# A two-layer decoder trunk: the RMSNorm channel sum split over four column groups of the array, with a second product that adds the groups

## What is computed

```python
def _rmsnorm(x, g):
    xf = x.astype(jnp.float32)
    y = xf * lax.rsqrt(jnp.mean(xf * xf, axis=-1, keepdims=True) + EPS)
    return (y * g.astype(jnp.float32)).astype(x.dtype)

def _modulate(x, g, shift, scale):
    return _rmsnorm(x, g) * (1 + scale[:, None, :]) + shift[:, None, :]

for layer in range(DEPTH):
    h = _modulate(x, norm_g[layer, 0], shift, scale)    # norm 0, norm 2
    x = x + gate[:, None, :] * mixer(h)
    h = _modulate(x, norm_g[layer, 1], shift, scale)    # norm 1, norm 3
    x = x + gate[:, None, :] * _hier_moe(h, ...)
return _rmsnorm(x, final_g)                             # norm 4
```

## Time and profile before

| | us |
|---|---|
| median of 3 runs | 1664.53 (1662.39 to 1671.16) |
| the profiled execution | 1674.01 |
| its span, first to last instruction | 1672.5 |
| TensorE matmuls busy | 1472.2 (88%) |
| weight loads busy | 1028.0 (61%) |
| VectorE busy | 620.4 (37%) |
| ScalarE busy | 413.5 (25%) |
| POOL busy | 225.0 (13%) |
| mean granted TensorE clock | 0.906 |

### The profile page before, as it was taken

One profiled execution on the slowest core, in us unless ns is written; L12 is line 12 of the kernel. 1 busy time (PEld: TensorE's weight loads), 2 busy tenths in 40 slices (PEclk: granted clock), 3 DMA queues, 4 the chain that ended last, 5 costly groups with the idle time before them and its releaser, 6 DMA issues.

```text
span 1672.5 us, 19460 instructions
## 1 busy us (share of the span) xinstructions
PE 1472.2 (88%) x7272; PEld 1028.0 (61%) x7272; DVE 620.4 (37%) x1426; ACT 413.5 (25%) x843; POOL 225.0 (13%) x206
## 2 busy tenths in 40 slices
PE   5698998969799999998369999999996899999945
PEld 3345586654388777775235677666544777777733
DVE  2795736541232421111252003888512324211113
ACT  4214112130312122221110113667404121222202
POOL 5001200000002010000534590000000110000010
PEclk8689998989868999999679999999997699999976
DMA  9543323341765789887683663000005176998941
GB/s 239 160 151 51 71 76 101 124 129 51 236 241 176 301 321 329 325 326 254 154 101 104 199 200 126 1 2 2 1 0 226 42 284 241 334 345 316 327 161 51
DMA packets 131928, 287.61 MB, mean 172 GB/s; under 512 B 11959, under 2 KB 94251, under 8 KB 120044
## 3 DMA queue, kind: packets, MB, share of 16 engines
q1 hardware_dynamic: 110112, 232.80, 40.8%
q0 software_dynamic: 13456, 25.12, 7.4%
q10 hardware_dynamic: 8268, 28.46, 4.2%
HBM read 269.94 MB, written 30.93 MB: 180 GB/s over the span
## 4 chain that ended last, share of the span: by engine, by line
PE 78%; DVE 10%; issue 4%; DMA 3%; ACT 3%; POOL 1%; ACTq 0%; DVEq 0%; POOLq 0%
PE bank L772 18%; PE bank L518 12%; PE bank L784 9%; PE bank L697 7%; PE bank L506 3%; PE bank L766 2%; PE bank L709 2%; PE bank L882 2%; PE bank L474 2%; PE bank L910 2%; PE bank L894 2%; PE bank L641 2%; PE bank L820 2%; PE bank L452 1%; PE bank L724 1%
## 5 line engine op out<-in xcount | busy, mean ns | idle before, releaser
L518 PE MATMUL bank<-hT,ring 128*128 128x512 f32 x448 | 201.8, 613 | 23.6 <-ACT hT L1014 13.4
L772 PE MATMUL bank<-ring,arena 128*128 128x256 f32 x800 | 177.9, 379 | 0.0
L518 PEld LDWEIGHTS bank<-hT,ring 128*128 128x128 f32 x448 | 87.7, 197 | 134.1 <-issue 109.5
L772 PEld LDWEIGHTS bank<-ring,arena 128*128 128x128 f32 x800 | 150.1, 190 | 19.4
L772 PE MATMUL bank<-arena 128*128 128x256 f32 x672 | 152.1, 383 | 0.0
L1818 DVE SCALAR_TENSOR_TENSOR arena<-bank,arena 128x256 f32<-128x256 f32 x46 | 22.3, 484 | 325.4 <-ACT arena L1180 325.1
L772 PEld LDWEIGHTS bank<-arena 128*128 128x128 f32 x672 | 128.1, 193 | 16.9
L2051 POOL DMA_INDIRECT arena<-h_tokens,arena x46 | 50.1, 1090 | 568.9 <-PE bank L766 359.0
L697 PE MATMUL bank<-mixT,ring 128*128 128x512 f32 x256 | 110.4, 593 | 1.6 <-ACT mixT L1137 0.9
L784 PE MATMUL bank<-ring,arena 128*128 128x512 f32 x224 | 100.8, 593 | 3.2 <-issue 3.2
L1172 ACT ACTIVATE arena<-bank 128x512 f32<-128x512 f32 x92 | 55.0, 597 | 178.8 <-PE bank L766 102.2
(11 more groups left out here) (427 smaller groups left out, 2186.7 us busy)
## 6 DMA issues: line engine op xcount, KB each, us to landing
ring<-in_ada_w SPq DMA_DIRECT2D x48, 1024.0 KB
ring<-in_e_w_down SPq DMA_DIRECT2D x28, 1024.0 KB
ring<-in_e_w_up SPq DMA_DIRECT2D x26, 1024.0 KB
ring<-in_e_w_gate SPq DMA_DIRECT2D x24, 1024.0 KB
expert_rows<-arena ACTq DMA_DIRECT2D x46, 512.0 KB, 8.3
arena<-in_e_w_gate SPq DMA_DIRECT2D x22, 1024.0 KB
arena<-in_e_w_up SPq DMA_DIRECT2D x20, 1024.0 KB
arena<-in_e_w_down SPq DMA_DIRECT2D x18, 1024.0 KB
```

Of the source, the lines that this page charges most:

```text
L518: last = mm(bank(stage, i)[:, :], chunk(kind, m, c)[:, k, j * P:(j + 1) * P], hT[:, k, :], start=(k == 0), stop=(k == KD - 1))
L772: last = mm(b[:, CC * n:CC * n + CC], xgT[:, e % 2, k, :], chunk(w, l, e)[:, k, :], start=(k == 0), stop=(k == KD - 1))
```

## The change

Each norm takes two banks instead of one. The first product keeps its 8 products of one square each, but with a stationary operand of 32 columns, `first`, whose first column is ones and whose other columns are zero. Product `k` goes to column group `k % 4`, that is to PSUM partitions `32*(k%4)` to `32*(k%4)+31`, so that four partial sums come to lie in rows 0, 32, 64 and 96 and zeros in all other rows. ScalarE copies the bank into `rstd` (`sums`). A second product of `ones` with `rstd`, 128x512, adds the four rows and spreads the sum over all partitions; VectorE's `variance` reads it from the second bank.

```diff
-STAGES = [("x", KD), ("param", 1), ("adap", 1), ("norm0", 1), ("adap", 1), ...
+STAGES = [("x", KD), ("param", 1), ("adap", 1), ("norm0", 2), ("adap", 1), ...
...   the same for norm1 to norm4
+        first = sb("first", [P, 32])
...
             def norm(m):
                 wait_bank(pe, f"norm{m}")
-                b = bank(f"norm{m}")
                 for k in range(KD):
                     pe.wait_ge(S["sq_ready"], KD * m + k + 1)
-                    last = mm(b[:, :], ones[:, :], hT[:, k, :], start=(k == 0), stop=(k == KD - 1))
+                    g = k % 4
+                    last = mm(bank(f"norm{m}")[32 * g:32 * g + 32, :], first[:, :], hT[:, k, :], start=(k < 4), stop=(k >= 4),
+                              skip_group_check=True)
                 last.then_inc(fsem(f"norm{m}"), 1)
+
+            def norm_sum(m):
+                wait_bank(pe, f"norm{m}", 1)
+                pe.wait_ge(S["sum_ready"], m + 1)
+                mm(bank(f"norm{m}", 1)[:, :], ones[:, :], rstd[:, :], start=True, stop=True).then_inc(fsem(f"norm{m}", 1), 1)
 
             ada_rows(0)
             norm(0)
             ada_rows(1)
+            norm_sum(0)
...
             norm(1)
+            norm_sum(1)
             ada_rows(14)
...   norm_sum(m) right behind norm(m) for 2, 3 and 4 too
+            def sums(m):
+                wait_full(act, f"norm{m}")
+                AC(rstd[:, :], bank(f"norm{m}")[:, :], ACT.Copy).then_inc(S["sum_ready"], 1)
+                act.wait_ge(S["sum_ready"], m + 1)
+                nc.scalar.nop().then_inc(rsem(f"norm{m}"), 1)
...
             ada_row(0)
+            sums(0)
             act.wait_ge(S["dve_s5"], 2)
...
                     AC(hT[:, k, :], xT[:, k, :], ACT.Square).then_inc(S["sq_ready"], 1)
+                sums(m)
                 act.wait_ge(S["var_ready"], m + 1)
...
-                wait_full(dve, st)
-                link(V.tensor_scalar(rstd[:, :], bank(st)[:, :], 1.0 / D, EPS, ALU.mult, ALU.add))
-                signal(rsem(st))
+                wait_full(dve, st, 1)
+                link(V.tensor_scalar(rstd[:, :], bank(st, 1)[:, :], 1.0 / D, EPS, ALU.mult, ALU.add))
+                signal(rsem(st, 1))
                 signal(S["var_ready"])
...
             link(G.memset(ones[:, :], 1.0))
+            link(G.memset(first[:, :], 0.0))
+            link(G.memset(first[:, 0:1], 1.0))
```

More of the change, by code:

```diff
@@ L44 @@
 MAGIC = 12582912.0
-STAGES = [("x", KD), ("param", 1), ("adap", 1), ("norm0", 1), ("adap", 1), ("ct", 2), ("fvec", 2), ("adap", 2), ("ada0", 1),
+STAGES = [("x", KD), ("param", 1), ("adap", 1), ("norm0", 2), ("adap", 1), ("ct", 2), ("fvec", 2), ("adap", 2), ("ada0", 1),
           ("u", 4), ("adap", 2), ("ada0g", 1), ("gates", 1), ("s5_e", 8), ("u2", 8), ("ut", 4), ("s5_g", 8), ("qk", 4),
@@ L54 @@
           ("mls", 1 + NT), ("adap", 1), ("o", 4), ("ada1_4", 1), ("mlh", 2), ("adap", 1), ("mly", 4), ("ada1_5", 1),
-          ("mlt", MH), ("aout", 8), ("adap", 2), ("norm1", 1), ("adap", 2)]
+          ("mlt", MH), ("aout", 8), ("adap", 2), ("norm1", 2), ("adap", 2)]
 NPRE = 8
@@ L88 @@
 WIDE = [sum(1 for x in STEPS[:n + 1] if x[1] > 1) for n in range(NI)]
-STAGES += [("norm2", 1), ("nkc", 4), ("ngate", 1), ("nq", 8), ("chid", 4), ("nks", 2), ("kcmp", 1), ("vcmp", 1), ("nvs", 4),
+STAGES += [("norm2", 2), ("nkc", 4), ("ngate", 1), ("nq", 8), ("chid", 4), ("nks", 2), ("kcmp", 1), ("vcmp", 1), ("nvs", 4),
            ("cscore", NT), ("nkw", 2), ("ctr", 2), ("nvw", 4), ("ctr", 2), ("ada3", 1)]
-STAGES += [("as", 2 * NI, (0, 1, 2, 3)), ("at", len(PTILE), (4, 5)), ("ao", NH // 2, (6, 7)), ("nout", KD), ("norm3", 1)]
+STAGES += [("as", 2 * NI, (0, 1, 2, 3)), ("at", len(PTILE), (4, 5)), ("ao", NH // 2, (6, 7)), ("nout", KD), ("norm3", 2)]
 STAGES += moe_stages(1) + moe_stages2(1)
-STAGES += [("norm4", 1), ("xo", 8)]
+STAGES += [("norm4", 2), ("xo", 8)]
 TILE, USES, _next = {}, [0] * 8, 0
@@ L304, in build @@
         free = [sem(f"bank_free{i}") for i in range(8)]
-        names = ["x_in", "raw_in", "dt_in", "c_in", "small_in", "twiddle", "rows_ready", "rows_used", "const_ready", "x_ready", "par_ready", "sil_ready", "mod_ready",
+        names = ["x_in", "raw_in", "dt_in", "c_in", "small_in", "twiddle", "rows_ready", "sum_ready", "rows_used", "const_ready", "x_ready", "par_ready", "sil_ready", "mod_ready",
                  "pow_ready", "e_ready", "et_ready", "g_ready", "m_in", "sq_ready", "h_part", "h_ready",
@@ L800, in _ @@
             norm(2)
+            norm_sum(2)
             pe.wait_ge(S["h_ready"], KD * 3)
@@ L916, in _ @@
             norm(3)
+            norm_sum(3)
             route(1)
@@ L919, in _ @@
             norm(4)
+            norm_sum(4)
             for i in range(8):
```

## The result

| | before | changed |
|---|---|---|
| median of 17 runs each | 1666.74 (1662.39 to 1679.96) | 1678.11 (1671.45 to 1680.74) |
| ratio, 95% interval | | 1.0047 [1.0027, 1.0067] |
| profiled execution / span | 1674.01 / 1672.5 | 1679.77 / 1677.9 |

A forecast was written before the change was run, and what follows sets the result against it. The chain of waits bounds the kernel, TensorE holding 78%. Gains of 3.2 + 1.9 + 0.3 + 0.3 in norms 1, 4, 3, 2, less 0.3 for memsets, give 5.4 us: 1664.53 to 1659.1, range 1653 to 1667.

The forecast's parts named there:

- The first product: Norm's 16 passes in column groups: 3.6 us at the low clock with squares ready; otherwise 4.7 (high) or 5.6 (low).
- the question of the waits: First product: assumed a product may start beside another group's although a wait on its square stands between; no row showed it.
- in order: Rival, chance 0.13: everything behind a waiting pass of the first product waits too, 9 slots instead of 4; gain 0.1, 1664.4.
- alone: Rival, chance 0.07: each wait lets a product start only when the array is empty; 10.2 us slower, 1674.7.
- Copy and second product: In each norm ScalarE's copy costs 0.8 us with handovers, the second product 1.03 (high clock) or 2.07 (low).
- Norm 0: 12 us of slack hide the sum; `sums(0)`, now ahead of the two Sin, stays just hidden, cost 0.
- Norms 3 and 4: Sum ends earlier: norm 3 by 0.3 us (0.6 gain to 0.5 loss), norm 4 by 1.9 (1.4 to 2.4).
- Norm 2: Sum ends 1.4 to 2.4 us earlier, but VectorE's operations meet POOL's; gain 0.3 us (-0.5 to +2.4).
- POOL gives way: Rival, chance 0.12: in norm 2 VectorE's eight operations keep their pace against POOL; norm 2 gains 4.6 us, 1654.8 in all.
- They still end about when the reciprocal does: Norm 1: TensorE's `ada_rows(14)` and `(15)`, 3.66 us behind the new wait, end with the reciprocal; norm 1 gain 3.2 us.
- Can the lower column work cost clock?: Asked of the norms' products; answer: work in four column groups raises the clock, second product taken as high half the time.
- 2 us either way: Expert stage: its 32 transposes and 64 gate products may meet either clock by luck, moving single norms by 2 us.

The follow-up runs named there:

- kept busy: Changed kernel plus 16 unread products of 128 columns between ada_rows(15) and the transposes after norm 1: 1664.94, ratio 0.9957 to the kernel before.
- paced: Changed kernel plus two unread products of 128 columns for each tile VectorE normalises in norms 1 and 3: 1660.6, ratio 0.9896 to the kernel before.
- the moved copies: Changed kernel with only ScalarE's ada_row(14) and ada_row(15) moved behind norm 1's shift: 1670.68, ratio 0.996 to the kernel before.
- the first two experiments: Changed kernel with norms 0, 2, 3 and 4 back in old form: 1680.03, ratio 1.004; with norm 1 alone back: 1666.64, ratio 0.9968, both to the kernel before.

## Why the prediction was wrong, point by point

- **The first product: right.** 16 passes took 3.55 us in norm 0, where all squares lay ready (predicted 3.6), 4.68 and 4.59 in norms 2 and 3 (4.7 to 5.6) and 5.46 in norm 4 (5.6). Norm 4 settles the question of the waits, since its squares came one by one and its whole stream ran at the low clock:

```profile
1649.80:1655.20 5.40, 5.40 (x16) 1.39 (x16) 0.00 (x0) 3.46 (x7) 0.00 (x0) 0.50 0.00 0
```

  The rival *in order* needs 6.8 us there and 7.7 in norm 0, and *alone* what the old form cost; both fall. Norms 2 and 3 wouldn't tell, because at the high clock nine slots (3.9 us) are shorter than the eight squares (4.27). The Trainium skill ("TensorE: Matmul & The Clock Gate", Part 3, The mechanism) has products start and end strictly in program order; the 3.55 us speak against it, since the two passes of each product share a group and order alone would make nine slots of them. The 4.3 us that the prediction estimated from the page's gain for three tiles are too slow as well.
- **Copy and second product: right.** 0.60 and 1.10 us, the latter high in all five norms, where I let it be high half the time.
- **Norm 0: right.** The Sin starts at 37.84, released by VectorE's queue; the table load had ended at 36.20. That is past 37, which I had named as a sign of being wrong, but `sums(0)` didn't hold it: the head is late as a whole, from the first parameter transpose on (22.01 against 20.30, the same 1.7 us as the Sin). The head's 433.2 us against 431.8 can't be told from chance: the same stretch took 429.9 to 433.7 in the four traces of the kernel before, and 432.6 to 434.3 in those of the changed one. The memsets do shift ScalarE's first parameter DMA, from 5.04 us in the traces with the old constants to 5.36; whether these 0.3 us reach the landing is not resolved, since the first parameter transpose started at 19.4 to 21.1 us in the four traces of the kernel before and at 21.5 to 22.0 in those of the changed one, but at 19.9 and 20.5 in two other kernels with the memsets.
- **Norms 3 and 4: right in kind, small in size.** Predicted 0.3 and 1.9, measured 0.7 and 2.5. Norm 4's gain depends on the clock that the old form met: the kernel with the new norm 1 alone kept the old norm 4, met the high clock there and took 18.5 us from the first square to the output transposes, as short as the new form (18.0 to 18.7 in the four traces of the changed kernel).
- **Norm 2: right, by the stated mechanism.** The sum came 3.3 us earlier after the first square and `amul` slipped in ahead of POOL (0.17 us instead of 2.22), so the eight L1345 started 4.9 us earlier after it. But then they met POOL's three operations, as the step says: 10.19 us instead of 5.96, and 0.7 us were left (predicted 0.3). *POOL gives way* falls. In two other kernels with this norm 2 (kept busy and paced) `amul` met POOL after all and the stretch took 24.0 us, no gain, which the step had as its other branch. The Trainium skill ("Advanced Engine Details and Errata", Mode Summary) notes that VectorE's second port is shared with GpSimd, so that GpSimd's instructions and VectorE's two-port ones block each other. The 4.2 us fit that; no run shows whether L1345 is a two-port one.
- **Norm 1: the step "They still end about when the reciprocal does" failed.** It looked at TensorE's work behind the new wait and not at the DMA ahead of that work. The sum came 4.9 us earlier (predicted 3.2) and the reciprocal ended at 448.40, but the chunk for `ada_rows(15)` landed at 450.32, 17.1 us after the first square, and the rows ended at 452.29, 3.9 us after the reciprocal. In the kernel before, that row's copy ended at 451.36, 1.6 us before the shift began: this was all the room there was. Measured 1.6 us against this trace and a loss of 0.2 against the two of the kernel before with 24.8; the moved copies gave 3.5 more.
- **What the sum left out: the stretch behind norm 1.** My question about the clock was put to the norm's own products only ("Can the lower column work cost clock?"). The risk behind it was in the last lines, sized at "2 us either way" and called luck. It had no term, no chance and no place in the range. It cost 6.3 us in routing and 4.3 in the experts. The stage is 208 passes that run at the pace of the clock, right behind a gap of 7.70 us, and rows I had read (0.50 at 472.6, 1.00 at 476.3) showed that the clock was changing inside it. That was the place to work out what it costs when the high times there are half as long: by the lengths above some 6.8 us, and 6.3 were measured.

The local gains of the norms are 1.6 + 0.7 + 0.7 + 2.5 = 5.5 us against a predicted 5.7 without the memsets. That is agreement by luck, since norm 1's share is half and norm 4's more. The base was a small error too: the forecast started from 1664.53, the median of three runs, and the median of 17 is 1666.74. From there the predicted gain gives 1661.3, still far from 1678.11.

**Shown:** the new norm 1 carries the loss (the first two experiments); in the changed kernel's traces the time goes into the routing stretch and the experts, at a lower granted clock with the same instructions, and the time at the low clock accounts for both; and in two traces of it (kept busy, paced) work on TensorE up to the transposes takes both away. **Open:** why the rise comes later behind the new form. The gap is shorter than the old one (5.90 against 7.70), but equal gaps of 5.90 gave 31.5, 28.3 and 25.1, and the kernel before gave 31.5 after 6.56 and 25.2 after 7.70. Nor does the clock at the gap's start decide it: the last row block ran at 1.93 us (low) in the changed kernel and at 1.07 (high) in the second trace of the kernel before, and both met 31.5. A rival stands untested: that only the moment decides at which the stretch begins, 0.6 us being enough, as in the pair 456.58 and 457.15. No run here moves the gap without changing the work around it. Why the experts of the changed kernel meet a second low piece is open as well. It doesn't simply follow routing: 283.3 followed 25.1 in the kernel with moved copies.

## What to carry to other kernels

When an edit shortens work on TensorE ahead of an idle gap, cost the stage behind the gap at both clock levels, and look in several executions at which level it meets; the difference can be larger than the edit's whole gain. Follow each engine that is in order through its next few waits and ask which release does not move with the edit, a DMA's landing above all. A few unread products paced by the tiles that the next stage waits for are a cheap cover for such a gap, and worth trying before and after the change. They are no guarantee: of the four kernels that had them, routing took 23.2 us in one, 23.1 in one, and 27.4 and 25.9 in the others.

## What the runs showed of the hardware

- Products of different column groups overlap over open semaphore waits: in norm 4, 16 passes whose squares came one by one over 4.26 us took 5.46 us at granted clock 0.50, where eight slots of 0.85 us behind the first pass would make 6.8. With all squares ready, norm 0 took 3.55 at 0.50.
- The same stretch of 208 passes (32 of transposes, 64 for the gates, 64 for the rows, 48 with a single column) takes from 23.2 to 31.5 us by the granted clock alone (mean 0.84 to 0.61), and one and the same kernel shows 25.2 and 31.5 in different executions. The experts behind it take 278.5 to 278.7 us plus half of their time at the low clock.
- VectorE and POOL working at the same time in norm 2 cost each other unevenly: eight L1345 took 4.2 us more than in the earlier trace rows, the two L2060 only 0.7 more (4.36 against 3.69).
